# Two transformer blocks in one kernel: a new order of steps and PSUM banks in the second block's feed-forward part

## The chip, the cores and the metric

One NeuronCore of a Trainium2 chip. The metric is the time of one execution on the device, in microseconds (us), median of several runs. The last stage of the kernel, the feed-forward part of the second block, is where the change lies.

## The reference, cut to what matters

The reference runs two blocks on x (512 tokens x 1024, float32). The change touches only the last lines of the second:

```python
h2 = rmsnorm(x, mlp_norm_w[l])
u = jax.nn.relu(jnp.einsum('bld,df->blf', h2, w_up[l]))      # 1024 -> 4096
x = x + jnp.einsum('blf,fd->bld', u * u, w_down[l])          # 4096 -> 1024
return rmsnorm(x, final_norm_w)
```

## The kernel before, in words

**Number format.** Every matrix is split into a high part (a rounded copy) and a low part (what the rounding left), and each product is three matmuls: high x high, high x low, low x high (function `three`, L812 to L816). TensorE (PE) multiplies, ScalarE (ACT) makes high parts, GpSimd (POOL) or VectorE (DVE) low parts, SyncE (SP) issues the loads.

**Quarters.** The 4096 hidden columns are cut in four quarters q = 0 to 3 of 1024. A quarter has four *units* of w_up_2, ("up", q, j), here u0 to u3: 256 hidden columns each, 48 matmuls into two PSUM banks (k = 0, 1). After each half DVE takes relu of the bank into `f2[q % 2]` (L2232) and ACT squares it in place (L1690). Units 0 and 1 give rows 0 to 3 of the quarter, units 2 and 3 rows 4 to 7.

**Products.** w_down of a quarter is multiplied by a Strassen-like scheme: blocks A11, A12, A21, A22 of the squared hidden values (rows 0-3 or 4-7, tokens in two halves), B11 to B22 of the weights, and *seven* products instead of eight, ("down", q, n), here d0 to d6: A11 B11, A12 B21, S1 T1, S2 T2, S4 B22, S3 T3, A22 T4. S3 = A11 - A21, S1 = S3 + A22, S2 and S4 are token sums (L2276 to L2284, S3 L2273); T1 to T4 weight sums (T1 L2251, T2 L2255, T3 L2259, T4 L2263), made in place over loaded blocks; all on DVE. A product is 24 matmuls into two banks. The products of a set form chains a (d0, d3, d5, d6), b (d1) and c (d2, d4): a chain goes on adding in its banks, and after each product DVE adds the running sum to x (the *take*, L2239). Chain a has banks 0 and 1 for even q and 6 and 7 for odd q, b has 2 and 3, c has 4 and 5. Before PE writes a bank again it waits until the last take from that bank is done (`claim_tail`, L1239).

**The order.** `STREAM` is the list of all 42 steps, and every engine walks it. In before it is: u2 u3 of q 0 (u0 and u1 of q 0 come ahead of the stream), the four units of q 1, the seven products of q 0 one after another (first set); then for q = 1 and 2 a set by `BETWEEN`, products of q mixed with units of q + 1; last the seven products of q 3. With "a set" the text means the products of one q and what is mixed with them. The step two places ahead is prepared at each step: ACT makes its token high part (`token_high`, L1682) and its weight high part (`tail_high`, L1666); the weight low part is POOL's in two halves (L797, L799) or, for d2, d3, d5 and d6, DVE's (`weight_low`, L2299); the token low part is DVE's (`token_low`, L2292). There are three slots for split weights and three for split token blocks.

**DVE's iteration.** At step v, in this order: the second take of step v-1; token sum S2 or S4 at d0 or d1; S3 two steps ahead of a set's d0, S1 one step ahead; T2, T3, T4 one step ahead of d2, d3, d4; token low and weight low of step v+2; T1 one step ahead of d0; the first take of step v. So a late wait in it delays the takes. ACT's iteration: second square of step v-1, token high and weight high of step v+2, first square of step v.

**Loads.** Five raw slots of 1 MB (two transfers of 512 KB each); `load_tail` (L705 to L724) asks for a load once the slot's former content has been split, and where a weight sum still reads it, once that sum is made: the slot of B11 is free after T4, which comes one step ahead of d4. SP's queue takes loads in the order of `STREAM`.

The order by steps (a bar begins a set; the units u1, u2 and u3 in the set of q are quarter q + 1's, and u0 at its end is quarter q + 2's; in the list `BETWEEN` that u0 opens the next group):

```
before  u02 u03 u10 u11 u12 u13 | d0 d1 d2 d3 d4 d5 d6 u20 | d0 d1 u1 d2 d3 u2 d4 u3 d5 d6 u0 | d0 d1 u1 d2 d3 u2 d4 u3 d5 d6 | d0 .. d6
```

Of the kernel before, what the change touches and what calls it, by code (L numbers as in the profile page):

```python
# [209 lines left out]
def completion_order():  # L210
# [3 lines left out]
    for phase, h in (("out1", "h2"), ("down1", "h3"), ("out2", "h4")):  # L214
# [4 lines left out]
        for n, t in enumerate(after):  # L219
# [7 lines left out]
FF2_Q = FF2 // 1024  # L227
# [3 lines left out]
OPENS = (0, 1, 2)  # L231
TO_X = ((0, 0), (0, 0), (2, 1), (0, 1), (0, 1), (2, 1), (2, 0))
VECTOR_LOW = (2, 3, 5, 6)
BETWEEN = (("up", 0), ("down", 0), ("down", 1), ("up", 1), ("down", 2), ("down", 3), ("up", 2), ("down", 4), ("up", 3),
           ("down", 5), ("down", 6))


def second_mlp():

    up = [[("up", q, j) for j in range(4)] for q in range(FF2_Q)]  # L240
    down = [[("down", q, n) for n in range(7)] for q in range(FF2_Q)]
    out = up[0][2:] + up[1] + down[0]
    for q in range(1, FF2_Q - 1):
        out += [up[q + 1][n] if kind == "up" else down[q][n] for kind, n in BETWEEN]
    return out + down[FF2_Q - 1]


STREAM = second_mlp()
AT = {step: v for v, step in enumerate(STREAM)}
RAW_SLOTS, W_SLOTS, A_SLOTS = 5, 3, 3  # L250
# [32 lines left out]
def tail_banks():  # L283

    out = []
    for kind, q, j in STREAM:
        for k in range(2):
            if kind == "up":
                out.append(2 + (2 * j + k) % 4)
            else:  # L290
                out.append({"a": 6 * (q % 2), "b": 2, "c": 4}[CHAIN[j]] + k)
    return out


TAIL_BANK = tail_banks()


# [21 lines left out]
def two_blocks(nc: bass.Bass, a, out: bass.AP):  # L319
# [11 lines left out]
    with ctx:  # L331
# [144 lines left out]
        def tokens_of(q, name):  # L476

            if name == "S3":
                return s3[:, :, :]
            k, t = {"A11": (0, 0), "S2": (0, 0), "A12": (1, 0), "S4": (1, 0), "A21": (0, 1), "S1": (0, 1),  # L480
                    "A22": (1, 1)}[name]
            return f2[q % 2][:, 4 * k:4 * k + 4, t * S // 2:(t + 1) * S // 2]
# [12 lines left out]
        def sem(name):  # L495
            return ctx.enter_context(nc.semaphore(name))
# [70 lines left out]
        squared = sem("squared")  # L567
# [728 lines left out]
        def _(act):  # L1296
# [287 lines left out]
            for kind, s in ACT_EVENTS:  # L1584
                if kind == "logits":
# [12 lines left out]
                    k = s - OTB_AT  # L1598
# [69 lines left out]
            def token_high(v):  # L1668

                kind, q, n = STREAM[v]  # L1670
                a_n = 7 * q + n
                name = PRODUCTS[n].split()[0]
                if name[0] == "A":
                    act.wait_ge(squared, 8 * q + 8)
                else:
                    act.wait_ge(tokens_added, 4 * q + TOKEN_SUMS.index(name) + 1)
                if a_n >= A_SLOTS:
                    before = AT["down", (a_n - A_SLOTS) // 7, (a_n - A_SLOTS) % 7]
                    act.wait_ge(tail_started, before + 2)
                else:  # L1680
                    act.wait_ge(tail_started, 1)
                nc.scalar.activation(a_hi[:, a_n % A_SLOTS, :, :], tokens_of(q, name), ACT.Copy).then_inc(a_hi_made, 1)  # L1682
# [15 lines left out]
            for at_v in range(N):  # L1698
                if at_v:
                    square(at_v - 1, 1)  # L1700
                if at_v + 2 < N:
                    if STREAM[at_v + 2][0] == "down":
                        token_high(at_v + 2)
                    tail_high(at_v + 2)
                square(at_v, 0)
# [26 lines left out]
        def _(dve):  # L1732
# [419 lines left out]
            for kind, s in DVE_EVENTS:  # L2152
                turn, h = s // HEADS, HEAD[s % HEADS]
                if kind == "logits":
# [16 lines left out]
                    k = s - OTB_AT - 1  # L2171
# [94 lines left out]
            def token_sum(q, name):  # L2266

                out = tokens_of(q, name)
                if name == "S3":
                    dve.wait_ge(squared, 8 * q + 8)  # L2270
                    if q:
                        dve.wait_ge(a_lo_made, 7 * (q - 1) + 6)
                    made = V.tensor_tensor(out, tokens_of(q, "A11"), tokens_of(q, "A21"), ALU.subtract)  # L2273
                elif name == "S1":
                    dve.wait_ge(tokens_added, 4 * q + 1)
                    made = V.tensor_tensor(out, out, tokens_of(q, "A22"), ALU.add)  # L2276
                elif name == "S2":
                    dve.wait_ge(tokens_added, 4 * q + 2)
                    dve.wait_ge(a_lo_made, 7 * q + 1)
                    made = V.tensor_tensor(out, tokens_of(q, "S1"), out, ALU.subtract)  # L2280
                else:
                    dve.wait_ge(tokens_added, 4 * q + 3)
                    dve.wait_ge(a_lo_made, 7 * q + 2)
                    made = V.tensor_tensor(out, out, tokens_of(q, "S2"), ALU.subtract)  # L2284
                made.then_inc(tokens_added, 1)
# [16 lines left out]
            for at_v in range(N - 1):  # L2302
                if at_v:
                    take(at_v - 1, 1)
                kind, q, n = STREAM[at_v]
                coming = next((c for c in range(FF2_Q) if AT["down", c, 0] - at_v in (1, 2)), None)
                if kind == "down" and n < 2:
                    token_sum(q, TOKEN_SUMS[2 + n])
                if coming is not None:
                    token_sum(coming, TOKEN_SUMS[2 - (AT["down", coming, 0] - at_v)])  # L2310
                nearest = STREAM[at_v + 1]
                if nearest[0] == "down" and 2 <= nearest[2] <= 4:
                    weight_sum(nearest[1], ADDS[nearest[2] - 1])
                if at_v + 2 < N and STREAM[at_v + 2][0] == "down":
                    token_low(at_v + 2)
                    if low_count(at_v + 2)[0]:
                        weight_low(at_v + 2)
                if coming is not None and AT["down", coming, 0] - at_v == 1:
                    weight_sum(coming, "T1")
                take(at_v, 0)  # L2320
# [90 lines left out]
```

## Time and profile before

| | us |
|---|---|
| median of 3 runs | 1594.5 (1593.4 to 1596.06) |
| the profiled execution, its own time | 1594.65 |
| its span, first to last instruction | 1592.9 |
| TensorE busy in the span | 1559.0 (98%) |
| VectorE busy | 935.2 (59%) |
| GpSimd busy | 713.9 (45%) |
| ScalarE busy | 532.2 (33%) |
| mean granted clock of TensorE | 0.994 of full |

Busy matmul time is no measure of progress by itself: matmuls are pipelined, and at a lowered clock they are longer. What counts is when a step starts, against the sum of the steps before it. Times in the text such as 1314.95 are us from the span's start. The stream starts at 1249.64 and the last matmul begins at 1585.56.

### The profile page before, as it was taken

What the parts mean: (1) busy time and instruction counts of PE and PEld (TensorE: products, weight loads), DVE (VectorE), ACT (ScalarE), POOL (GpSimd) and SP (SyncE); (2) the same over time, 40 slices, a digit from 0 to 9 for tenths busy, and PEclk for the clock granted to TensorE, in tenths of its full rate; (3) what the DMA queues carried; (4) which work ended last, traced back from release to release, by engine and by line L of the source; (5) the groups of instructions that cost most, each with busy time, mean ns of one, the idle gap of its engine ahead of it and who ended that gap; (6) DMA issues with size and microseconds to landing.
All of it is one profiled execution on the core that took longest, in us unless ns stands there. A gap on an engine that the chain in (4) does not pass through costs nothing.

```text
span 1592.9 us, 19236 instructions
## 1 busy us (share of the span) xinstructions
PE 1559.0 (98%) x7495; PEld 1283.3 (81%) x7495; DVE 935.2 (59%) x1197; ACT 532.2 (33%) x760; POOL 713.9 (45%) x265
## 2 busy tenths in 40 slices
PE   9999999999999999999999999999999999989996
PEld 7887788888888988888888887876788887778775
DVE  5901588910256566666005389988564129957678
ACT  3012211200134444344124344247443334333334
POOL 5874189677861354454442002421251442545431
PEclk9999999999999999999999999999999999999999
DMA  6232032232333333333223222321133512241211
GB/s 225 84 128 79 1 113 79 89 123 83 102 107 105 99 87 105 95 89 106 106 80 114 81 80 80 104 56 28 46 123 108 175 53 90 69 159 38 97 51 53
DMA packets 127382, 147.00 MB, mean 92 GB/s; under 512 B 5143, under 2 KB 98375, under 8 KB 127304
## 3 DMA queue, kind: packets, MB, share of 16 engines
q1 hardware_dynamic: 125430, 141.05, 27.8%
q10 hardware_dynamic: 1874, 4.85, 1.0%
q8 instruction: 55, 0.90, 0.2%
q14 instruction: 23, 0.19, 0.0%
HBM read 143.79 MB, written 2.10 MB: 92 GB/s over the span
## 4 chain that ended last, share of the span: by engine, by line
PE 89%; DVE 5%; issue 3%; ACT 1%; POOL 1%; DVEq 0%; POOLq 0%; ACTq 0%
PE ps L814 27%; PE ps L816 27%; PE ps L815 27%; PE ps L969 3%; PE ps L1044 2%; PE ps L1211 1%; DVE x L2239 1%; DVE a_lo L2292 1%; PE ps L1032 1%; DVE w_lo L2299 1%; PE ps L1228 1%; POOL w_hi L756 1%; PE ps L1103 1%; ACT w_hi L1666 0%; PE ps L1065 0%
## 5 line engine op out<-in xcount | busy, mean ns | idle before, releaser
L761 POOL TENSOR_TENSOR w_lo<-raw,w_hi 128x1024 fp32r<-128x1024 f32 x166 | 420.5, 2554 | 495.9 <-ACT w_hi L1314 493.2
L814 PE MATMUL ps<-hT_hi,w_hi 128*128 128x512 f32 (+1 forms) x848 | 327.1, 386 | 9.7 <-DVE x L2239 8.4
L815 PE MATMUL ps<-hT_lo,w_hi 128*128 128x512 f32 (+1 forms) x848 | 325.6, 384 | 0.0
L816 PE MATMUL ps<-hT_hi,w_lo 128*128 128x512 f32 (+1 forms) x848 | 325.1, 383 | 0.0
L814 PEld LDWEIGHTS ps<-hT_hi,w_hi 128*128 128x128 f32 x848 | 160.6, 189 | 44.1 <-issue 11.5
L756 POOL TENSOR_TENSOR w_hi<-raw,cells 128x2048 fp32r<-128x2048 f32 x35 | 129.6, 3701 | 126.4 <-PE ps L814 125.1
L816 PEld LDWEIGHTS ps<-hT_hi,w_lo 128*128 128x128 f32 x848 | 160.7, 189 | 31.3
L815 PEld LDWEIGHTS ps<-hT_lo,w_hi 128*128 128x128 f32 x848 | 160.7, 189 | 30.4
L1314 ACT ACTIVATE w_hi<-raw 128x2048 fp32r<-128x2048 f32 (+1 forms) x58 | 109.6, 1890 | 128.2 <-PE ps L814 106.4
L814 PE MATMUL ps<-w_hi,hT_hi 128*128 128x512 f32 (+2 forms) x400 | 151.6, 379 | 0.5 <-POOL w_lo L780 0.5
L815 PE MATMUL ps<-w_lo,hT_hi 128*128 128x512 f32 (+2 forms) x400 | 150.1, 375 | 0.0
L816 PE MATMUL ps<-w_hi,hT_lo 128*128 128x512 f32 (+2 forms) x400 | 150.0, 375 | 0.0
L1789 DVE TENSOR_TENSOR w_lo<-raw,w_hi 128x1024 fp32r<-128x1024 f32 (+1 forms) x20 | 22.0, 1144 | 144.4 <-ACT w_hi L1314 144.4
L814 PEld LDWEIGHTS ps<-w_hi,hT_hi 128*128 128x128 f32 x400 | 75.4, 188 | 14.0 <-POOL w_lo L780 0.9
L816 PEld LDWEIGHTS ps<-w_hi,hT_lo 128*128 128x128 f32 x400 | 75.3, 188 | 13.2
L815 PEld LDWEIGHTS ps<-w_lo,hT_hi 128*128 128x128 f32 x400 | 75.4, 189 | 12.7
L797 POOL TENSOR_TENSOR w_lo<-raw,w_hi 128x1024 fp32r<-128x1024 f32 x10 | 25.8, 2582 | 122.7 <-ACT w_hi L1666 122.6
L814 PE MATMUL ps<-w_hi,a_hi 128*128 128x512 f32 x152 | 60.4, 398 | 6.6 <-DVE x L2239 2.3
L2232 DVE TENSOR_SCALAR f<-ps 128x512 f32<-128x512 f32 x28 | 18.9, 688 | 76.2 <-PE ps L816 76.2
L816 PE MATMUL ps<-w_hi,f_lo 128*128 128x512 f32 x160 | 62.3, 390 | 0.0
L814 PE MATMUL ps<-w_hi,f_hi 128*128 128x512 f32 x160 | 62.3, 390 | 0.0
L815 PE MATMUL ps<-w_lo,f_hi 128*128 128x512 f32 x160 | 62.3, 389 | 0.0
(367 smaller groups left out, 3077.2 us busy)
## 6 DMA issues: line engine op xcount, KB each, us to landing
raw<-in_w_in SPq DMA_DIRECT2D x86, 512.0 KB, 4.6
raw<-in_w_up SPq DMA_DIRECT2D x68, 512.0 KB, 4.7
raw<-in_w_down SPq DMA_DIRECT2D x30, 512.0 KB, 4.3
raw_tail<-in_w_down SPq DMA_DIRECT2D x24, 512.0 KB, 5.9
raw<-in_w_out SPq DMA_DIRECT2D x16, 512.0 KB, 4.2
raw<-in_w_ret_o SPq DMA_DIRECT2D x8, 512.0 KB, 4.1
raw<-in_w_sgu_o SPq DMA_DIRECT2D x8, 512.0 KB, 4.0
raw_tail<-in_w_up SPq DMA_DIRECT2D x8, 512.0 KB, 4.9
```

The costliest lines, as they stand in the source:

```text
L756: nc.gpsimd.tensor_tensor(hi[:, 0:n], raw[:, s, 0:n], zero.broadcast_to([P, n]), ALU.add).then_inc(unit_hi, 1)
L761: nc.gpsimd.tensor_tensor(lo[:, c], raw[:, s, c], hi[:, c].bitcast(f32), ALU.subtract).then_inc(unit_split, 1)
L797: nc.gpsimd.tensor_tensor(lo[:, 0:UNIT // 2], tail_raw_of(v)[:, 0:UNIT // 2], hi[:, 0:UNIT // 2].bitcast(f32), ALU.subtract)
L814: first = nc.tensor.matmul(dst, a_hi, b_hi, start=start, stop=False, skip_group_check=onto)
L815: nc.tensor.matmul(dst, a_hi, b_lo, start=False, stop=False, skip_group_check=onto)
L816: return first, nc.tensor.matmul(dst, a_lo, b_hi, start=False, stop=stop, skip_group_check=onto)
L969: last = nc.tensor.transpose(ps[:, BANK[t], n * width:n * width + width], src, ident[0:k, 0:k])
L1032: nc.tensor.matmul(bank(t), kT[:, h, mb * P:(mb + 1) * P], qT[:, h, :], start=True, stop=True).then_inc(psum_ready, 1)
L1044: last = nc.tensor.matmul(ps[:, BANK[t], nn * 256:nn * 256 + 256], sT[:, h % 2, mb, n0:n0 + P], v[:, mb, h * RET_DV:(h + 1) * RET_DV], sta ...
L1314: nc.scalar.activation(slot_of(u)[0][:, 0:n], raw[:, s, 0:n], ACT.Copy).then_inc(hi_given, 1)
L1789: V.tensor_tensor(lo[:, c], raw[:, u % 2, c], hi[:, c].bitcast(f32), ALU.subtract).then_inc(unit_split, 1)
L2232: V.tensor_scalar(f2[q % 2][:, c, :], ps[:, TAIL_BANK[e], :], 0.0, None, ALU.max).then_inc(tail_taken, 1)
```

## The change

It replaces the order of the first set: the units of q 1 (u11, u12, u13) now stand among the products of q 0, by the same list `BETWEEN` as the other sets. In that list unit 3 moves from between d4 and d5 to between d5 and d6. The banks of the units change: unit 0 keeps 2 and 3; units 1 to 3 of quarter q use `6 * (q % 2)`, chain a's pair of their own quarter (6 and 7 for q 1 and 3, 0 and 1 for q 2), which the running set of quarter q - 1 does not use; in before unit 1 and 3 had 4 and 5, unit 2 had 2 and 3. The units u2 and u3 of q 0 have 2, 3 and 4, 5, as before. Two waits on squares are cut to what is read: A11 and S3 = A11 - A21 wait for four squares of the quarter, where they waited for eight, and S1, which reads A22, gets a wait for all eight.

```
after   u02 u03 u10 | d0 d1 u1 d2 d3 u2 d4 d5 u3 d6 u0 | d0 d1 u1 d2 d3 u2 d4 d5 u3 d6 u0 | d0 d1 u1 d2 d3 u2 d4 d5 u3 d6 | d0 .. d6
```

```diff
-BETWEEN = (("up", 0), ("down", 0), ("down", 1), ("up", 1), ("down", 2), ("down", 3), ("up", 2), ("down", 4), ("up", 3),
-           ("down", 5), ("down", 6))
+BETWEEN = (("up", 0), ("down", 0), ("down", 1), ("up", 1), ("down", 2), ("down", 3), ("up", 2), ("down", 4), ("down", 5),
+           ("up", 3), ("down", 6))
...
-    out = up[0][2:] + up[1] + down[0]
-    for q in range(1, FF2_Q - 1):
+    out = up[0][2:]
+    for q in range(FF2_Q - 1):
         out += [up[q + 1][n] if kind == "up" else down[q][n] for kind, n in BETWEEN]
...
-                out.append(2 + (2 * j + k) % 4)
+                out.append((2 + 2 * (j % 2) if q == 0 else 2 if j == 0 else 6 * (q % 2)) + k)
...
-                    act.wait_ge(squared, 8 * q + 8)
+                    act.wait_ge(squared, 8 * q + (4 if name == "A11" else 8))
...
                 if name == "S3":
-                    dve.wait_ge(squared, 8 * q + 8)
+                    dve.wait_ge(squared, 8 * q + 4)
...
                 elif name == "S1":
+                    dve.wait_ge(squared, 8 * q + 8)
                     dve.wait_ge(tokens_added, 4 * q + 1)
```

## Rows read from the trace of the kernel before

**Rows 1.** The page: busy time of PE, and the chain that ended last.
```profile
PE 1559.0 (98%) x7495; PEld 1283.3 (81%) x7495; DVE 935.2 (59%) x1197; ACT 532.2 (33%) x760; POOL 713.9 (45%) x265
...
PE 89%; DVE 5%; issue 3%; ACT 1%; POOL 1%; DVEq 0%; POOLq 0%; ACTq 0%
```

**Rows 2.** Windows from 1249.64 on, cut at the sets; columns in the first line.
```profile
core 0: us, PE busy (x) PEld busy (x) DVE busy (x) ACT busy (x) POOL busy (x), PEclk, DMA share, GB/s
1249.64:1314.95 65.31, 65.31 (x291) 54.10 (x290) 15.13 (x17) 20.32 (x20) 29.92 (x12) 1.00 0.39 129
1314.95:1369.07 54.12, 51.13 (x218) 41.55 (x217) 51.69 (x34) 22.74 (x16) 25.80 (x8) 0.97 0.28 98
1369.07:1459.19 90.12, 85.34 (x361) 69.45 (x360) 61.89 (x42) 31.93 (x26) 39.82 (x14) 0.96 0.28 94
1459.19:1537.67 78.48, 73.16 (x314) 59.54 (x313) 54.25 (x39) 30.13 (x25) 28.03 (x11) 0.98 0.24 81
1537.67:1585.95 48.28, 41.28 (x169) 32.12 (x167) 47.05 (x39) 19.29 (x22) 13.94 (x4) 0.96 0.06 22
...
1250.00:1270.00 20.00, 20.00 (x90) 16.56 (x89) 2.61 (x4) 6.14 (x6) 9.49 (x4) 1.00 0.79 263
```

**Rows 3.** Timeline of PE: start, duration, instruction, [idle before it <- releaser].
```profile
1339.65 0.47 PE L814 MATMUL ps<-tail_hi,a_hi 128*128 128x512 f32 x1 [2.78 <-DVE x L2239]
...
1391.91 0.47 PE L814 MATMUL ps<-w_hi,a_hi 128*128 128x512 f32 x1 [0.56 <-DVE f L2232]
...
1423.59 0.77 PE L814 MATMUL ps<-hT_hi,w_hi 128*128 128x512 f32 x1 [4.19 <-DVE x L2239]
...
1470.70 0.50 PE L814 MATMUL ps<-hT_hi,w_hi 128*128 128x512 f32 x1 [0.47 <-POOL w_lo L799]
```

**Rows 4.** Window over unit 3 of the second set.
```profile
1423.59:1437.43 13.84, 13.84 (x48) 11.17 (x49) 4.69 (x4) 2.54 (x2) 0.00 (x0) 0.78 0.57 203
```

**Rows 5.** Timelines of PE, DVE, SP, ACT and POOL around unit 3's load.
```profile
1402.91 0.39 PE L814 MATMUL ps<-hT_hi,tail_hi 128*128 128x512 f32 x1
...
1403.79 3.75 DVE L2263 TENSOR_TENSOR raw_tail<-raw_tail,raw 128x2048 f32<-128x2048 f32 x1
...
1407.62 2.02 SPq L724 DMA_DIRECT2D raw<-in_w_up  x4
...
1412.97 1.92 ACT L1666 ACTIVATE w_hi<-raw 128x2048 fp32r<-128x2048 f32 x1 [13.09 <-DMA raw<-in_w_up]
...
1417.33 3.36 POOL L799 TENSOR_TENSOR w_lo<-raw,w_hi 128x1024 fp32r<-128x1024 f32 x1
...
1422.76 1.40 DVE L2239 TENSOR_TENSOR x<-ps,x 128x512 f32<-128x512 f32 x2
```

**Rows 6.** Timeline of DVE: token low, alone and beside POOL; token sum; weight sum.
```profile
1529.52 1.22 DVE L2292 TENSOR_TENSOR a_lo<-f,a_hi 128x1024 fp32r<-128x1024 f32 x1
...
1446.65 3.42 DVE L2292 TENSOR_TENSOR a_lo<-f,a_hi 128x1024 fp32r<-128x1024 f32 x1
...
1550.47 1.22 DVE L2284 TENSOR_TENSOR f<-f 128x1024 f32<-128x1024 f32 x1
1551.60 2.28 DVE L2255 TENSOR_TENSOR raw<-raw_tail,raw 128x2048 f32<-128x2048 f32 x1
```

**Rows 7.** Timelines of ACT, PE and DVE around the last set's start.
```profile
1527.71 0.63 ACT L1690 ACTIVATE f<-f 128x512 f32<-128x512 f32 x1 [4.81 <-DVE f L2232]
...
1532.71 1.06 ACT L1682 ACTIVATE a_hi<-f 128x1024 fp32r<-128x1024 f32 x1 [1.47 <-PE ps L814]
1533.68 1.90 ACT L1666 ACTIVATE w_hi<-raw_tail 128x2048 fp32r<-128x2048 f32 x1
...
1544.86 0.51 PE L814 MATMUL ps<-w_hi,a_hi 128*128 128x512 f32 x1 [1.59 <-POOL w_lo L799]
...
1555.87 2.29 DVE L2299 TENSOR_TENSOR w_lo<-raw,w_hi 128x2048 fp32r<-128x2048 f32 x1 [0.85 <-ACT w_hi L1666]
```

## The prediction, made before the changed kernel was run

> **What bounds the kernel now.** I read the page first: TensorE (PE) is busy 98% of the span and makes up 89% of the chain that ended last [rows 1], so time can only come from holes in its stream. Then the windows view of the last stage, cut where a set of products begins [rows 2]. Six units of w_up_2 in a row take 65.31 us without a hole: 10.885 us a unit of 48 matmuls, 5.44 us a product of 24. Against these, the stretches after it lose:
> - first set (7 products, 1 unit): 54.12 - 48.98 = 5.1
> - second set (7 products, 4 units): 90.12 - 81.64 = 8.5
> - third set (7 products, 3 units): 78.48 - 70.75 = 7.7
> - last set (7 products): 48.28 - 38.10 = 10.2
>
> That is 31.5 us. The PE timeline says what ends the holes [rows 3]. In the first set product 4 waits 2.78 us for the take of product 2, which holds the same banks; DVE is busy 51.69 of 54.12 us there [rows 2], because seven products follow each other and each brings it takes, sums and low parts. In the second set unit 3 of q 2 waits 4.19 us for the take of product 4, the step just before it, in banks 4 and 5; the third set has a twin of it. Product 2 waits 0.56 us for the unit before it, banks 4 and 5 again, and also has a twin. Unit 1 of the third set waits 0.47 us for POOL's low part. A hole of several us costs a second time: over the unit after the 4.19 us the granted clock is 0.78 of full, part of it spent at the 1.2 GHz level, and the unit takes 13.84 us for 10.885 [rows 4]: 3.0 us more.
>
> **What the change does, part by part.**
> Order and banks, sets one to three. A set becomes d0 d1 u1 d2 d3 u2 d4 d5 u3 d6 u0, also the first (q 0). In before the last users of a bank pair were one or two steps back where the holes are; now I find for each step, counted along the new order: d4 reuses d2's banks 3 steps later, u3 those of u2 3 steps later, d6 those of d5 with u3 between, d2 those of a step 5 or 8 back, u1, u2, d3, d5 and d0 3 or more back. Two steps apart are u0 and d1 (as before, no hole there) and, at the end, u3 and the last set's d0, with a whole product between. So every wait of [rows 3] that names a take goes. What remains is data: is each step's low part, load and token part there in time?
>
> - Unit 3. Its raw slot is freed by weight sum T4, on DVE at the start of unit 2. In before: unit 2 starts at 1402.91, T4 ends 1407.54, the load is issued at 1407.62, ACT starts the high part at 1412.97 and POOL ends the low part at 1420.69 [rows 5], 17.8 us after unit 2 began. In before unit 3 was due 16.3 us after it, so with free banks alone 1.5 us would stay. Now d5 lies between as well: due at 21.8, spare 4.0 us. Cost 0. Behind this late load ACT held back d5's token and high part (DVE then waited, and finished its takes at 1424.2 [rows 5]); in the new order d5's parts stand ahead of that wait in ACT's queue, so that queueing goes too.
> - Unit 1 after d0 and d1. POOL's low part was late by 0.47 us, because DVE's takes of u0 came late, behind S3, S1 and T1, each drawn out by POOL. In the new order u0's low part is made under u3 and is done before d6 begins, where in before it came under d5 and d6, so two of the six POOL halves leave that stretch. I take 0.1 us a set; the far bound is the 0.47.
> - DVE load. A mixed set holds the same instructions as the second set of before, whose DVE time is 61.89 us [rows 2] in what is now 81.64 us (76%). For the first set this load was squeezed into 48.98.
> - First set's start. d0 is now step 3, not 6. S3 and d0's token part need only the four squares made before the stream (the wait is lowered to 4). Its loads B11, B21, B12, B22 (4 MB) join the burst after 1250; at 263 GB/s [rows 2] they take 16 us, here by 1266. T1 wants B11 and B12 when u10 runs, at 1271; T2 wants B22 at 1293. Then unit 1's load, behind them in SP's queue (1 MB, 4 us), by 1270, wanted at 1282. Cost 0, spare 5 us.
>
> All three sets at their sum of steps: -21.3 us. For small remainders (0.1 us three times, and an unforeseen half-step of DVE) I add 0.5.
>
> The wait that is added. S1 now waits itself for all eight squares, and DVE's d1 token part, T1 and the takes of the next unit are queued behind it. In the first set S1 runs under u10 and d1 is due 16 us after u03's end; in the next two u3 lies two steps back. Before the last set u3 is followed by d6 alone, 5.44 us. I walk it from u3's start = 0: PE ends u3 at 10.9, d6 at 16.3; d0 of the last set 16.3, d1 due 21.8, d2 27.2, d3 32.6. DVE's second take of u3 11.8, ACT's square (0.63) 12.4, token part of d1 (1.06) 13.4, high part (1.90) 15.3 [rows 7]; DVE: S1 13.6, low of the token 14.9, T1 17.1 (1.22, 1.22 and 2.28 us if alone [rows 6]). POOL's two halves for d1 wait for T1 and then alternate with S2: 2.4 + 1.1 + 2.3 us, so end at 22.9: d1 stalls 1.1 us, where before it stalled 1.59 [rows 7]. DVE goes on: S2 20.5, d2's parts 26.1, takes 27.5, S4 28.7, T2 30.9, d3's token 32.1, and waits 0.8 us for ACT as before [rows 7], so that d3's low part starts at 32.9, 16.6 us after d0 began. In before it started at 1555.87, 18.2 us after d0 (1537.67). From there on both kernels do the same with DVE full, so I carry the difference to the end: -1.6 us.
>
> Here trace and skill bear on each other. Row first: a DVE operation with both inputs in SBUF takes 1.22 us alone and 3.42 us when POOL is at work, 2.2 us or one POOL half more [rows 6]; takes, which read PSUM, stay at 0.7 a piece [rows 5]. The Trainium skill, SBUF — State Buffer, Who interferes with whom, states that the two share a port pair that is an exclusive lock, and that the one issued second fully blocks. The trace agrees. By that rule units, whose low parts are POOL's, are bad company for products. What that would come to here is worked out from rows as the third rival.
>
> **Sum.** -21.3 + 0.5 - 1.6 = -22.4 us. The profiled execution took 1594.65 us (span 1592.9), 0.15 above the median of 1594.5; against the median that gives 1572.1, so 1572.
>
> **Rivals.**
> 1. The last set gains more (0.15). If POOL's halves for d1 fall into the gaps of DVE, d1 doesn't stall, d2's parts end 3 us earlier, and with a smaller hole before d3 the clock may stay up. Then 5 us of the 10.2 go: 1594.5 - 21.3 - 5 = 1568. Against it: T1 and the first POOL half are issued 0.4 us apart.
> 2. Each mixed set keeps something (0.17): DVE behind by S3, S1 and T1 at u0, POOL's low part of unit 1 late, or T4 so late that u3's spare of 4.0 us is used up. Lower bound one hole of 0.5 a set (+1.4); upper bound one hole like that of product 4, 2.78 us with the clock after it, some 3 us more than forecast a set (+9). That gives 1574 to 1581.
> 3. DVE becomes the bound and it gets slower (0.03). Mechanism: the shared port, in every set. A set has 19 DVE operations with both inputs in SBUF (7 token lows, 4 weight lows, 4 weight sums, 4 token sums). Alone with the takes they need 7 x 1.22 + 8 x 2.28 + 4 x 1.22 + 11 x 1.40 = 47.1 us [rows 5, 6]. If all 19 waited out a POOL half of 2.2 us, 41.8 more make 88.9, 7.2 over the 81.64; three sets lose 21.7, and with three falls of the clock [rows 4] 9 more: 30.7 - 21.3 = 9.4 us slower than before, 1604. It decides once DVE needs over 81.64 a set. Against it: POOL has only 14 halves in a set [rows 2], so 47.1 + 30.8 = 77.9 is the most, and the second set showed 61.89.
> 4. No difference (0.02): DMA or another fixed date sets the end, so that sets done earlier wait in the last one. Against it: its loads are asked for by steps of the stream and follow it, and DMA is at 0.06 in the last stretch [rows 2].
>
> **How the numbers follow.** Forecast 0.63, likeliest range 1570.5 to 1574; rivals 0.15, 0.17, 0.03, 0.02. The range goes from rival 1's 1568, less half a us, to rival 2's upper bound, 1581. Everything but rivals 3 and 4 is faster by far over 0.2% (3.2 us, about what can be told here from no change): faster 0.95, within 0.02, slower 0.03.
>
> **What would show it.** Right: d0 of the last set starts near 1516.3 to 1517 (before 1537.67); between 1249.64 and there no PE wait over 0.5 us and the clock at 1.00; first set's products spread over 76 us with DVE under 80%; unit 3 waits for nothing. d1 of the last set still waits for POOL about 1 us. Wrong: PE waits for POOL's or DVE's low part at u1 or u3 (rival 2); DVE busy over 95% in a mixed set (rival 3); the last set's stretch at 44 us (rival 1) or over 50.

## The result and the profile after

| | before | changed |
|---|---|---|
| median | 1594.65 us (1593.4 to 1596.06, 4 runs) | 1572.09 us (1571.8 to 1573.28, 4 runs) |
| the profiled execution, its own time | 1594.65 us | 1571.8 us |
| its span | 1592.9 us | 1570.0 us |
| PE busy in the span | 98% | 99% |

The ratio is 0.986, 95% interval 0.9843 to 0.9877: 22.6 us faster, where 22.4 were forecast. The median of before is 0.15 us above the 1594.5 of the three runs that the prediction started from, since a fourth run is counted in.

First the windows view of the changed kernel, cut again where a set's first product starts. Columns as in [rows 2]: the stretch, its length, then busy us of PE, PEld, DVE, ACT and POOL with their counts, the granted clock, DMA's share and GB/s.

```profile
1250.00:1282.66 32.66, 32.66 (x146) 27.04 (x145) 10.99 (x11) 11.22 (x11) 15.74 (x6) 1.00 0.46 162
1282.66:1364.26 81.60, 81.60 (x361) 67.59 (x360) 56.84 (x41) 31.77 (x26) 36.69 (x14) 1.00 0.31 104
1364.26:1445.86 81.60, 81.60 (x361) 67.59 (x360) 57.44 (x41) 32.36 (x27) 38.25 (x15) 1.00 0.31 103
1445.86:1516.58 70.72, 70.72 (x313) 58.58 (x312) 52.22 (x38) 30.50 (x25) 28.70 (x12) 1.00 0.26 90
1516.58:1562.88 46.30, 40.82 (x169) 32.07 (x167) 44.85 (x38) 18.95 (x22) 13.09 (x4) 0.96 0.06 23
```

Read the second column against the third: in the first three sets PE is busy for every microsecond, at a clock of 1.00, and each stretch is as long as its steps (81.64, 81.64 and 70.75 by the prediction's sum). Together with the three units ahead of them they run from 1250.00 to 1516.58, 266.6 us; the same 35 steps took 288.0 us before, from 1249.64 to 1537.67 [rows 2]. So 21.4 us are won here. The last set takes 46.30 us instead of 48.28: 2.0 more. DVE has the same work in a mixed set as in the second set of before and is busy for 57 us of 81.6, where it took 61.89 of 90.12 there [rows 2], so it has room.

The waits view of the changed kernel for PE, over the whole stream; in the kernel before the same list came to 20.1 us.

```profile
PE ps L814 <- DVE x L2239: 3.7, 2, 3.3
PE ps L814 <- DVE w_lo L2300: 1.0, 1, 1.0
PE ps L814 <- POOL w_lo L799: 0.8, 1, 0.8
```

All four of these holes lie in the last set. The timeline of PE shows them at products 1, 3, 4 and 6; before, there were five, at products 1, 3, 4, 5 and 6, the first of 1.59 us [rows 7].

```profile
1522.94 0.50 PE L814 MATMUL ps<-w_hi,a_hi 128*128 128x512 f32 x1 [0.75 <-POOL w_lo L799]
...
1535.16 0.50 PE L814 MATMUL ps<-w_hi,a_hi 128*128 128x512 f32 x1 [1.05 <-DVE w_lo L2300]
...
1544.22 0.76 PE L814 MATMUL ps<-w_hi,a_hi 128*128 128x512 f32 x1 [3.33 <-DVE x L2239]
...
1557.20 0.47 PE L814 MATMUL ps<-w_hi,a_hi 128*128 128x512 f32 x1 [0.35 <-DVE x L2239]
```

The timelines of DVE and POOL in the changed kernel show how the last set is entered: the weight sum T1 (L2251) begins before POOL's half and stays at 2.28 us, while the half (L797) is drawn out to 3.89; and product 3's low part (the row at 1532.82) starts 16.2 us after the set's first product.

```profile
1512.73 1.23 DVE L2277 TENSOR_TENSOR f<-f 128x1024 f32<-128x1024 f32 x1 [0.70 <-ACT f L1690]
1513.88 1.22 DVE L2293 TENSOR_TENSOR a_lo<-f,a_hi 128x1024 fp32r<-128x1024 f32 x1
1515.01 2.28 DVE L2251 TENSOR_TENSOR raw_tail<-raw,raw_tail 128x2048 f32<-128x2048 f32 x1
1515.68 3.89 POOL L797 TENSOR_TENSOR w_lo<-raw,w_hi 128x1024 fp32r<-128x1024 f32 x1 [6.75 <-ACT w_hi L1666]
...
1532.82 2.29 DVE L2300 TENSOR_TENSOR w_lo<-raw_tail,w_hi 128x2048 fp32r<-128x2048 f32 x1 [0.85 <-ACT w_hi L1666]
...
1536.35 3.81 DVE L2259 TENSOR_TENSOR raw<-raw_tail,raw 128x2048 f32<-128x2048 f32 x1
1540.09 3.39 DVE L2293 TENSOR_TENSOR a_lo<-f,a_hi 128x1024 fp32r<-128x1024 f32 x1
1543.40 1.41 DVE L2239 TENSOR_TENSOR x<-ps,x 128x512 f32<-128x512 f32 x2
```

In the kernel before, T1 of this set came 0.4 us after the set's start, when a POOL half was already under way, and took 4.49 us:

```profile
1538.08 4.49 DVE L2251 TENSOR_TENSOR raw<-raw_tail,raw 128x2048 f32<-128x2048 f32 x1
```

From product 3's start on the two kernels are alike, as the prediction assumed: 27.34 us to the last matmul in both. The hole before product 4 is 3.33 us instead of 1.71 only because product 3 ran at a clock of 1.00 and no longer at the lowered one; from product 3's start to product 4's it is 9.06 and 9.07 us. PE has to wait there for DVE in either case.

### The profile page after: what moved, and what is told of

It is laid out like the page before. It is cut to its first block, busy times and chain, and to the rows that moved or that the text cites. A ratio compares the mean times of both kernels' runs of the same rounds, so it can differ in the third digit from the quotient of the medians.

```text
span 1570.0 us, 19240 instructions
## 1 busy us (share of the span) xinstructions
PE 1550.6 (99%) x7495; PEld 1279.1 (81%) x7495; DVE 927.8 (59%) x1197; ACT 532.9 (34%) x760; POOL 708.8 (45%) x265
## 4 chain that ended last, share of the span: by engine, by line
PE 90%; DVE 3%; issue 2%; POOL 2%; ACT 1%; DMA 1%; DVEq 0%; SPq 0%; POOLq 0%; ACTq 0%
PE ps L814 28%; PE ps L816 27%; PE ps L815 27%; PE ps L969 3%; PE ps L1044 2%; PE ps L1211 1%; POOL w_lo L761 1%; PE ps L1032 1%; PE ps L1228 1%; POOL w_hi L756 1%; PE ps L1103 1%; DVE x L2239 0%; PE ps L1065 0%; DVE a_lo L2293 0%; DMA raw<-in_w_up 0%
## 5 line engine op out<-in xcount | busy, mean ns | idle before, releaser
L761 POOL TENSOR_TENSOR w_lo<-raw,w_hi 128x1024 fp32r<-128x1024 f32 x166 | 420.4, 2554 | 496.2 <-ACT w_hi L1314 493.5
L797 POOL TENSOR_TENSOR w_lo<-raw_tail,w_hi 128x1024 fp32r<-128x1024 f32 x13 | 33.6, 2584 | 97.6 <-ACT w_hi L1666 97.6
L1478 ACT ACTIVATE taps<-ps,conv 128x512 f32<-128x512 f32 x44 | 34.0, 773 | 83.5 <-PE ps L816 83.5
```

The lines of the kernel that those rows point to most:

```text
L761: nc.gpsimd.tensor_tensor(lo[:, c], raw[:, s, c], hi[:, c].bitcast(f32), ALU.subtract).then_inc(unit_split, 1)
L797: nc.gpsimd.tensor_tensor(lo[:, 0:UNIT // 2], tail_raw_of(v)[:, 0:UNIT // 2], hi[:, 0:UNIT // 2].bitcast(f32), ALU.subtract)
L1478: nc.scalar.activation(taps[:, j % 2, c, :], bank(t + c), ACT.Identity, bias=conv[:, 3, bass.ds(col, 1)], scale=conv[:, 1, bass.ds(col, 1) ...
```

## The experiments

The experiments ask whether the parts of the sum are the right ones: are the banks the cure, or the place of unit 3, or the mixing of the first set? And is the last set DVE's, as the walk through it assumed? Times are medians; a kernel is set against the changed one at 1572.1 us. The experiments ran in three groups, each with its own runs of before, whose medians were 1593.7 us (only the banks, only the order, first set unmixed, unit 3's old place), 1594.89 (the late load, the two edits of the last set and both together) and 1594.24 (the others). So a difference of under 1 us between kernels of two groups says nothing by itself.

### Only the banks

The kernel before with one line of the change:

```diff
-                out.append(2 + (2 * j + k) % 4)
+                out.append((2 + 2 * (j % 2) if q == 0 else 2 if j == 0 else 6 * (q % 2)) + k)
```

> The order of before with the new banks for the units. Theory 1 (each hole has its own cause: a bank for some, data for others): the first set keeps its 5.1 us and the last its 10.2; in sets two and three unit 3 no longer waits for product 4's take but still for its own low part, 1.5 us instead of 4.2 and without most of the 3 us of low clock, and product 2's 0.56 us goes. That is 11 to 13 us faster than before, 1581.5 to 1583.5. Rival (mixing and the even load of DVE are what pays, banks are incidental): within 3 us of before, 1591 to 1595.

Measured: 1579.84 us, against 1593.7 for before in the same group, ratio 0.9911 (0.9894 to 0.9928): 13.9 us faster, more than theory 1 allowed. No hole at all is left at unit 3. The trace tells why the 1.5 us for the late low part didn't stay. The timeline of this kernel, DVE, SP and POOL:

```profile
1403.37 2.28 DVE L2263 TENSOR_TENSOR raw_tail<-raw_tail,raw 128x2048 f32<-128x2048 f32 x1
...
1405.73 2.02 SPq L724 DMA_DIRECT2D raw<-in_w_up  x4
...
1412.97 2.42 POOL L797 TENSOR_TENSOR w_lo<-raw,w_hi 128x1024 fp32r<-128x1024 f32 x1 [5.06 <-ACT w_hi L1666]
1415.33 2.42 POOL L799 TENSOR_TENSOR w_lo<-raw,w_hi 128x1024 fp32r<-128x1024 f32 x1
```

In [rows 5] the fourth weight sum took 3.75 us beside POOL and the last POOL half 3.36 beside DVE. Here they take 2.28 and 2.42, and unit 3's low part is done at 1417.75, 15.2 us after unit 2 began at 1402.50 and 1.1 ahead of the 16.3 at which unit 3 is due. Once a hole goes, the engines meet each other at other moments, and a lateness measured beside the hole isn't the one left without it.

### Only the order

The changed kernel with the old line for the banks.

> The order of the changed kernel with the banks of before. Theory 1: with product 5 between product 4 and unit 3 the old banks are free in time too, and only product 2 waits again for the unit ahead of it, 0.5 to 0.7 us in each of three sets: 1573.5 to 1575. Rival (the free banks are what pays): the 4.2 us holes at unit 3 stay in some form, 1580 or more.

Measured: 1572.11 us, ratio 0.9865 (0.9848 to 0.9881): the changed kernel's time. Theory 1 was right that the place of unit 3 is enough, and wrong about product 2, which has the banks of the unit ahead of it again and doesn't wait. DVE and PE in this kernel, second set:

```profile
1384.54 0.68 DVE L2232 TENSOR_SCALAR f<-ps 128x512 f32<-128x512 f32 x1
...
1385.94 0.39 PE L814 MATMUL ps<-w_hi,a_hi 128*128 128x512 f32 x1
```

DVE's relu of unit 1's first half (L2232) ends at 1385.22, 0.7 us before product 2 wants that bank. PE has no hole here, so unit 1 began 10.88 us before 1385.94, at 1375.06, and DVE got to its first half 9.5 us after that. Before, product 2 waited 0.56 us for that relu [rows 3], which means that it came more than 10.88 us after the unit began. The dependence is there, but DVE is no longer behind.

### The fourth corner

First set mixed, but neither cure: the old banks, and unit 3 between products 4 and 5.

> First set mixed, unit 3 between products 4 and 5, and the banks of before: the fourth corner to the runs that changed only place or only banks. Theory 3 (free banks and the place behind product 5 are two cures of one hole, and either is enough): with neither, unit 3 waits for product 4's take in three sets, 4.2 us and 2 to 3 us of clock each, less the part that the low part costs anyway: 1588 to 1597. Rival (once the first set is mixed the holes are a matter of data alone): within 2 us of the same order with the new banks, 1577 to 1579.

Measured: 1596.34 us, ratio to before 1.0013 (1.0004 to 1.0023). The mixed first set brings nothing by itself: it trades its own 5.1 us for a third hole at a unit 3, and is 2.1 us slower than before. PE's timeline, first and second set:

```profile
1336.33 0.77 PE L814 MATMUL ps<-hT_hi,tail_hi 128*128 128x512 f32 x1 [4.62 <-DVE x L2239]
...
1426.64 0.49 PE L814 MATMUL ps<-hT_hi,w_hi 128*128 128x512 f32 x1 [4.33 <-DVE x L2239]
```

### Unit 3 back in its old place

```diff
-BETWEEN = (("up", 0), ("down", 0), ("down", 1), ("up", 1), ("down", 2), ("down", 3), ("up", 2), ("down", 4), ("down", 5),
-           ("up", 3), ("down", 6))
+BETWEEN = (("up", 0), ("down", 0), ("down", 1), ("up", 1), ("down", 2), ("down", 3), ("up", 2), ("down", 4), ("up", 3),
+           ("down", 5), ("down", 6))
```

> The changed kernel with unit 3 back between products 4 and 5. Theory 1: banks are free, but unit 3's low part is late by some 1.5 us in each of the three sets (its load is asked for after the fourth weight sum), so 3 to 6 us slower than the changed kernel, 1575 to 1578, PE waiting there for POOL and not for DVE. Rival (the hole was the bank alone): 1572 to 1573.

Measured: 1577.23 us, ratio to before 0.9895 (0.9879 to 0.9912), so 5.1 us slower than the changed kernel. The sum is as expected, its parts are not. PE waits for unit 3's low part in the first set alone, 1.68 us, where the fourth weight sum takes 4.29 us and the last POOL half 3.34 (2.28 and 2.41 in the second set); 0.47 and 0.44 us are lost at unit 1; and in the last set the holes before products 1 and 3 grow from 0.75 and 1.05 to 1.45 and 2.19 us. That is 4.4 us in all. The rest is lost at the edges of the holes, near 0.3 us at each of the first three, beside what PE's idle time shows; the clock stays at 1.00 after all of these. The waits view of this kernel:

```profile
PE ps L814 <- DVE x L2239: 3.5, 2, 3.3
PE ps L814 <- DVE w_lo L2300: 2.2, 1, 2.2
PE ps L814 <- POOL tail_lo L799: 2.1, 2, 1.7
PE ps L814 <- POOL w_lo L799: 1.9, 2, 1.4
```

With these the four corners of place and banks, all with the first set mixed and the finer waits, stand together (medians in us):

| | old banks | new banks |
|---|---|---|
| unit 3 before product 5 | 1596.3 | 1577.2 |
| unit 3 behind product 5 | 1572.1 | 1572.1 |

The two are cures of one hole. The place alone does it all; the banks alone do most; once the place is changed the banks add nothing that shows.

The last set's 2.0 us belong to unit 3's place too. From its first product to the last matmul it takes 47.89 us in the kernel before and 47.94 with the new banks; 47.75 to 47.78 in the three kernels that have the finer waits but unit 3 in its old place; and 45.92 to 45.96 in the three that have unit 3 behind product 5, whatever the banks and the first set. So 0.1 us is the finer waits' and some 1.8 the place's.

### The first set unmixed again

```diff
-    out = up[0][2:]
-    for q in range(FF2_Q - 1):
+    out = up[0][2:] + up[1] + down[0]
+    for q in range(1, FF2_Q - 1):
```

> The changed kernel with the first set unmixed again (three units of quarter 1 ahead of seven products in a row). Theory 1: the first set loses its 5.1 us again and nothing else moves: 1577 (1576.5 to 1578). Rival (the first set's backlog of DVE also spoiled the sets behind it): 1580 or more.

Measured: 1577.65 us, ratio 0.9899 (0.9882 to 0.9915): 5.6 us slower than the changed kernel, against 5.1 by the windows of before. In place of one hole of 2.78 us and one of 0.20 there are three, 2.78, 1.16 and 0.41 us, all behind DVE's takes; the second and third set are free of holes. More holes don't mean more time lost: in the kernel before the clock fell after the 2.78 us and here it did not, and from product 4's start to product 6's both take 12.97 us (more on this in the last section).

### The finer waits on squares alone

The kernel before, with the three changed lines that wait on `squared`.

> The kernel before with the finer waits on squares alone. Both theories of the sets: in the old order units stand far enough ahead that only S3 of the last set saves its 0.7 us of waiting for ACT, so within 1 us of before, 1593.5 to 1595. Rival (the waits on all eight squares held DVE back in every set and are part of the gain): 2 us or more faster.

Measured: 1594.43 us, ratio 1.0001 (0.9992 to 1.0011). No difference. In the mixed order they could not be left out: S3 of the first and last set stands in DVE's stream ahead of the second take of the unit whose squares the old wait asks for. This follows from the order of the steps; no run shows it.

### Unit 3's load asked for later

```diff
+                    if kind == "up" and name == 3:
+                        sp.wait_ge(tail_started, AT["down", q - 1, 4] + 1)
```

> The changed kernel, but the load of unit 3 is asked for only when product 4 has started, some 5.6 us later than now. In the changed kernel's trace the low part of unit 3 ends 2.7 us ahead of its start. Theory 1 (the load is the next thing to bind): holes of 1.5 to 2.5 us before unit 3 in each of three sets, with the clock after them, 5 to 11 us slower than the changed kernel, 1577 to 1583. Rival (the high part waits for ACT's second square of unit 2 anyway, so that the load has more room than the prediction gave it): under 3 us slower.

Measured: 1583.14 us, ratio 0.9926 (0.9911 to 0.9942), 11.0 us slower than the changed kernel. PE's waits in this kernel:

```profile
PE ps L816 <- POOL w_lo L801: 5.6, 3, 2.5
PE ps L816 <- DVE x L2241: 3.7, 2, 3.3
PE ps L816 <- POOL tail_lo L801: 2.4, 1, 2.4
```

Unit 3 waits 2.39, 2.41 and 2.50 us for POOL in the three sets, 7.3 us. The clock falls after the first two, to a mean of 0.85 and 0.84 over the unit, which with the edges of the hole costs some 1.9 us each; after the third, the longest, it stays at 1.00. The load was issued 0.3 us after product 4's start, where the changed kernel has it 5.6 us ahead, so it came 5.9 us later and left a hole of 2.4: its room was 3.5 us. So the load is what binds next, and the room is small. In the changed kernel itself the prediction's 4.0 us between the low part's end and unit 3 was too much, since ACT takes unit 3's high part only behind the second square of unit 2. ACT and POOL of the changed kernel, unit 3 of the second set, which starts at 1418.66:

```profile
1408.71 0.63 ACT L1690 ACTIVATE f<-f 128x512 f32<-128x512 f32 x1 [2.01 <-DVE f L2232]
1409.25 1.90 ACT L1666 ACTIVATE tail_hi<-raw 128x2048 fp32r<-128x2048 f32 x1
...
1413.58 2.40 POOL L799 TENSOR_TENSOR tail_lo<-raw,tail_hi 128x1024 fp32r<-128x1024 f32 x1
```

It ends at 1415.98, 2.7 us early, as it does in the other two sets.

### How much room the mixed sets have for POOL

POOL makes the first half of each of its low parts in sets one to three twice.

```diff
+                if AT["down", 0, 0] <= v < AT["down", FF2_Q - 1, 0] - 1:
+                    nc.gpsimd.tensor_tensor(lo[:, 0:UNIT // 2], tail_raw_of(v)[:, 0:UNIT // 2],
+                                            hi[:, 0:UNIT // 2].bitcast(f32), ALU.subtract).then_inc(twice, 1)
+                    doubled += 1
+                    pool.wait_ge(twice, doubled)
```

> The changed kernel, but POOL makes the first half of each of its low parts in sets one to three twice (21 halves of 2.4 us more, 7 a set). It tests how much room the mixed sets have, for the prediction's rival of the shared port. Port theory: DVE's busy time in a set goes from 57 us towards 70, its single operations get longer and PE gets holes behind DVE. Latency theory: DVE stays below 65, and what makes holes is POOL's own lateness, by 2.4 us and more at unit 1 and product 1, PE waiting there for POOL. By either 1576 to 1592; if the sets have room for it, under 1575.

Measured: 1610.69 us, ratio to before 1.0104 (1.0088 to 1.0119); worse than either theory had it. The window over its second set, and PE at unit 1:

```profile
1368.17:1467.76 99.59, 87.93 (x362) 70.99 (x360) 67.85 (x42) 32.26 (x26) 65.25 (x22) 0.93 0.25 85
...
1386.48 0.80 PE L821 MATMUL ps<-hT_hi,tail_hi 128*128 128x512 f32 x1 [5.24 <-POOL tail_lo L806]
```

PE waits for POOL's low parts 12 times over the stream, 26.8 us, and in sets one to three never for DVE, though DVE's busy time has gone from 57.4 to 67.9 us: its operations are drawn out beside POOL's (the low part before this hole took 4.46 us for 2.28) and POOL's beside them (4.39 for 2.40). Both theories were half right. The holes are POOL's lateness, and the lateness is 2.4 us of extra work, made longer where the two engines meet. The mixed sets have little room for more work on POOL.

### The last set: one low part moved to DVE

```diff
-    by_vector = [kind == "down" and n in VECTOR_LOW for kind, _, n in STREAM]
+    by_vector = [kind == "down" and (n in VECTOR_LOW or (q, n) == (FF2_Q - 1, 4)) for kind, q, n in STREAM]
```

> The changed kernel, but the weight low part of product 4 of the last set is made by DVE and not by POOL. Theory 2 (in the last set DVE is full and each POOL half next to it costs it more than the work itself): DVE's T3, token low of product 4 and this low part take 2.28 + 1.22 + 2.28 = 5.8 us instead of 3.81 + 3.39 = 7.2, product 4's hole goes from 3.3 to 1.9 us, and 1.4 to 2.5 us are gained: 1569.5 to 1570.7. Rival (what counts is how much work DVE has): 2.3 us more on a full DVE, 1574 to 1574.5.

Measured: 1570.33 us, ratio 0.9847 (0.9833 to 0.986), 1.8 us faster than the changed kernel. DVE of this kernel; compare the first two rows with the 3.81 and 3.39 us at 1536.35 and 1540.09 above.

```profile
1536.63 2.28 DVE L2259 TENSOR_TENSOR raw<-raw_tail,raw 128x2048 f32<-128x2048 f32 x1
1538.83 1.22 DVE L2293 TENSOR_TENSOR a_lo<-f,a_hi 128x1024 fp32r<-128x1024 f32 x1
1539.97 2.28 DVE L2300 TENSOR_TENSOR w_lo<-raw_tail,w_hi 128x2048 fp32r<-128x2048 f32 x1
1542.17 1.41 DVE L2239 TENSOR_TENSOR x<-ps,x 128x512 f32<-128x512 f32 x2
```

A full DVE was given 2.28 us more work and reached the takes that product 4 waits for 6.73 us after product 3 began (1535.44) instead of 8.24, 1.5 us earlier. The rival, which counts work alone, falls.

### The last set: T1 in DVE's idle time

```diff
-                if coming is not None and AT["down", coming, 0] - at_v == 1:
+                if coming is not None and coming < FF2_Q - 1 and AT["down", coming, 0] - at_v == 1:
                     weight_sum(coming, "T1")
                 take(at_v, 0)
+                if at_v == AT["down", FF2_Q - 1, 0] - 2:
+                    weight_sum(FF2_Q - 1, "T1")
```

> The changed kernel, but T1 of the last set is made in DVE's idle time in the second half of unit 3 instead of after S1. Theory 2: 2.3 us leave DVE's full stretch and the last set ends 2 to 3.5 us earlier: 1568.5 to 1570. Rival (the last set hangs on the loop from PE through the takes and ACT, not on the sum of DVE's work): within 0.5 us of the changed kernel.

Measured: 1570.59 us, ratio 0.985 (0.9837 to 0.9864), 1.5 us faster, under what theory 2 gave. The DVE timeline shows the part that was not won:

```profile
1509.14 2.29 DVE L2251 TENSOR_TENSOR raw_tail<-raw,raw_tail 128x2048 f32<-128x2048 f32 x1 [1.79 <-POOL w_lo L799]
...
1516.93 0.69 DVE L2239 TENSOR_TENSOR x<-ps,x 128x512 f32<-128x512 f32 x1 [1.16 <-PE ps L816]
```

T1 fits into the idle time, but now DVE waits 1.16 us for product 6 of the set before, to which it was late until now. Of 2.3 us 1.2 are given back there; the token sum behind it, 1.71 us instead of 2.11, brings the gain to the 1.5. The loop through PE does bind for a moment, as the rival said.

### Both, and one more

Both edits together:

> Both edits of the last set together. Theory 2: the gains add, as both shorten the same full stretch of DVE, 1566.5 to 1568.5. Rival (once DVE is relieved PE's own sum or another wait binds): no better than the better of the two.

Measured: 1568.66 us, ratio 0.9836 (0.9822 to 0.9849), 3.4 us faster than the changed kernel: 1.8 + 1.5 = 3.3, so they add. Then also the first take of product 1 ahead of the low part for which ACT is waited for:

```diff
                     token_low(at_v + 2)
+                    if STREAM[at_v + 2] == ("down", FF2_Q - 1, 3):
+                        take(at_v, 0)
                     if low_count(at_v + 2)[0]:
                         weight_low(at_v + 2)
```

> Both edits of the last set, and DVE makes the first take of product 1 while it would wait 0.85 us for ACT's high part ahead of product 3's low part. Theory 2 (the last set ends with the sum of DVE's work): 0.5 to 0.8 us faster than both edits alone, 1567.8 to 1568.2. Rival (DVE's sum no longer sets the end): no difference.

Measured: 1568.02 us (1567.86 to 1569.57), ratio to before 0.9839 (0.9826 to 0.9852); the hole at product 4 is 1.09 us instead of 1.82, and in the profiled executions the span is 0.7 us shorter. The medians are 0.6 us apart, in the expected range. But the two kernels ran in different groups, and each is 26.2 us faster than before in its own group; one of the five runs (1569.57) is slower than all of the kernel with both edits alone (1568.41 to 1568.76). So a gain of this last step is not shown. Either version beats the changed kernel.

## Why the prediction was right

**The sets, -21.3 us.** Right, by its own working: 48.98, 81.64 and 70.75 us were the sums of steps, and the windows show PE without a hole. They gave 21.4. The 0.5 us added for remainders was not needed.

**The total** came closer than its parts, by luck. In the profiled executions the sets and the last set gain 21.4 + 2.0 = 23.4 us, 1.0 more than the 22.4 forecast. Of this 0.4 is lost ahead of the stream, which starts at 1250.00 instead of 1249.64, and 0.2 behind the last matmul; and the profiled execution of the changed kernel lies 0.3 us below its median.

**The reason given for unit 3** was only half of it. The prediction named the bank, and counted steps since its last user with the new order and banks together, without asking which of the two was needed. The four corners tell: either ends the hole, and the order alone gives everything. The title's banks are not what this kernel's time comes from. The side sum "with free banks alone 1.5 us would stay" failed for the order of before: nothing stayed, because the stretch of the fourth weight sum and of POOL's half, taken from the trace with the hole, went with it. With the first set mixed 1.68 us did stay in that set, and nothing in the other two.

**Unit 3's spare of 4.0 us** was 2.7: the step missed that ACT has the second square of unit 2 in front of the high part. The conclusion, cost 0, held; the late load shows that the room is real and small.

**Unit 1.** Forecast 0.1 us a set, measured none.

**The last set, -1.6 us.** Measured -2.0. The walk's marks were forecast from unit 3's start, which was at 1500.26: product 1's stall 1.1 us, measured 0.75; DVE's S2 done at 20.5, measured 20.4; DVE's low part for product 3 16.6 us after the set's start, measured 16.2; the same 0.85 us of waiting for ACT. That the gain is carried to the end unchanged held to 0.01 us (27.34 us from product 3 on in both). That DVE is full there, and that POOL's halves beside it cost it more than their work, is shown by the low part moved to DVE. The sum of 10.2 us lost in the last set counts lowered clock and holes together; rival 1 hoped for time from a clock that stays up, and there is none to be had there, as the last section shows.

**Rivals.** DVE as the bound, drawn out by POOL (slower), did not come: DVE 57 us of 81.6 in a mixed set. But the doubled POOL halves show that this rival was not idle: half again as much POOL work costs 38.6 us over the changed kernel, though PE then waits for POOL and not for DVE as the rival had it. That the last set gains more did not come by itself; it came with two edits, 3.4 us of the 4 by which the rival's 1568 lay below the forecast. That the mixed sets keep something fell: no hole is left in them.

**What is left open.** How a hole of the same length can leave the clock alone in one kernel and lower it in another (below).

## What to carry to other kernels

When a step waits for a bank, list what frees it and what else stands between: moving a ready step in front is as good as another bank, and here better, since it gave the late load and DVE time as well. Change order and banks one at a time before crediting either. And a lateness read from a trace with a hole in it holds the hole's own effects; where two engines draw out each other's operations, as DVE and POOL here, the durations after the cure depend on whether they still meet, so take both as bounds. On a full DVE, taking work over from POOL can shorten the whole. And before a lowered clock is counted as a cost, ask what PE would have waited for at full clock.

## What was not expected of the hardware

The clock after short holes isn't decided by their length alone. The plainest pair is product 4 of the first set, unmixed in both kernels: PE idles 2.78 us before it in the kernel before and in the changed kernel with the first set unmixed. In the first the mean clock over the next 12.97 us is 0.87, in the second it stays at 1.00. The windows from product 4's start to product 6's, first of the kernel before:

```profile
1339.65:1352.62 12.97, 12.77 (x48) 10.07 (x49) 12.82 (x12) 5.84 (x4) 3.31 (x1) 0.87 0.69 246
```

```profile
1340.09:1353.06 12.97, 11.40 (x48) 8.85 (x49) 12.83 (x12) 5.85 (x4) 3.55 (x1) 1.00 0.71 247
```

The last set has such a pair too. With one low part moved, PE idled 1.78 us before product 4 and the clock stayed; with both edits it idled 1.82 us and the clock fell to the 1.2 GHz level within the product. The PE timeline and the window over the product, first of the kernel with one edit, then of the one with both:

```profile
1542.99 0.47 PE L814 MATMUL ps<-w_hi,a_hi 128*128 128x512 f32 x1 [1.78 <-DVE x L2239]
...
1542.99:1548.72 5.73, 5.72 (x24) 4.40 (x24) 5.73 (x4) 3.07 (x3) 0.00 (x0) 1.00 0.02 3
```

```profile
1541.29 0.47 PE L814 MATMUL ps<-w_hi,a_hi 128*128 128x512 f32 x1 [1.82 <-DVE x L2239]
...
1541.29:1548.00 6.71, 6.71 (x23) 5.36 (x24) 6.71 (x5) 3.07 (x3) 0.00 (x0) 0.75 0.01 2
```

What PE did over the products before (holes of 0.75 and 1.01 us in the first, 0.66 in the second) doesn't explain it in an obvious way.

And the fall costs nothing in either pair. The first two windows are equally long, 12.97 us: at full clock PE waits 1.16 and 0.41 us for DVE before products 5 and 6, and at the lowered one 0 and 0.20. In the last set, from product 4's start to the last matmul takes 18.31 us with the clock at 1.00 (one edit) and 18.31 with the fall (both), and 18.27 in the kernel before; the steps alone would take 16.3. DVE is busy for 12.8 of the 12.97 us and sets the pace, so a slower PE only fills its own waiting. It is otherwise where PE is the bound: the unit after the 4.19 us took 3.0 us too long [rows 4], and those after the first two holes of the late load 1.9 us each.
